# Gate rows, key roots and the gate bias of an attention layer: moved from the tail and from in front of attention into its first iteration, on one Trainium2 core

## The reference

```python
for i in range(DEPTH):
    mod = silu(c) @ w_ada[i] + b_ada[i]
    sh1, sc1, g1, sh2, sc2, g2 = split(mod, 6)
    h = rmsnorm(x, norm_mix[i]) * (1 + sc1) + sh1
    m = mla_mixer(h, ...) if i % 2 == 0 else rglru_mixer(h, ...)
    x = x + g1 * m
    h = rmsnorm(x, norm_ffn[i]) * (1 + sc2) + sh2
    x = x + g2 * moe(h, *route(h, ...), w_gu[i], w_dn[i])
```

## Time and profile before

| what | us |
|---|---|
| median of 3 runs | 1702.48 |
| fastest, slowest | 1700.49, 1705.16 |
| profiled execution | 1700.49 |
| span in the profile | 1698.7 |
| PE busy | 1384.3 (81%) |
| DVE busy | 686.6 (40%) |
| ACT busy | 347.9 (20%) |
| POOL busy | 296.6 (17%) |

### The profile page before, as it was taken

How to read it: one execution, slowest core, us unless ns; L and a number is a source line. 1 busy time by engine, 2 the same in 40 slices (tenths; PEclk the granted TensorE clock), 3 DMA queues, 4 the chain that set the end, 5 groups by cost and what they waited for, 6 DMA issues and landing times.

```text
span 1698.7 us, 33153 instructions
## 1 busy us (share of the span) xinstructions
PE 1384.3 (81%) x14067; PEld 803.0 (47%) x14067; DVE 686.6 (40%) x1316; ACT 347.9 (20%) x708; POOL 296.6 (17%) x340
## 2 busy tenths in 40 slices
PE   3999999989876777897757999797887768699754
PEld 3644554445644344485424444343564435377432
DVE  5677777766211111122205288757321112122113
ACT  3346555121100000001002345423010001001000
POOL 1001211000222032222100122200131222122200
PEclk9999999989988788999978999897998879899887
DMA  9654232599999999999996121066899999999997
GB/s 366 251 203 168 85 108 75 190 350 419 366 398 398 414 383 408 394 395 401 428 395 240 57 81 62 0 251 244 324 400 397 402 407 383 403 389 402 423 424 299
DMA packets 66841, 517.29 MB, mean 305 GB/s; under 512 B 13277, under 2 KB 26102, under 8 KB 49034
## 3 DMA queue, kind: packets, MB, share of 16 engines
q1 hardware_dynamic: 51696, 493.77, 73.2%
q0 software_dynamic: 10848, 16.24, 2.9%
q10 hardware_dynamic: 4154, 5.18, 0.9%
HBM read 506.27 MB, written 22.04 MB: 311 GB/s over the span
## 4 chain that ended last, share of the span: by engine, by line
PE 52%; DMA 33%; DVE 7%; another core or an unknown queue 2%; issue 2%; ACT 2%; SPq 1%; PEldq 1%; DVEq 0%; ACTq 0%
DMA ring_gu<-in_moe_w_gu_dram 29%; PE ps L1192 16%; PE ps L1199 6%; PE ps L1082 6%; DMA ring_gu<-in_w_ada_dram 4%; PE ps L1117 3%; PE ps L999 3%; PE ps L1101 2%; PE ps L909 2%; PE ps L1141 2%; PE ps L1019 2%; PE ps L973 2%; PE ps L889 2%; PE ps L937 2%
## 5 line engine op out<-in xcount | busy, mean ns | idle before, releaser
L1192 PE MATMUL ps<-ring_gu,arena 128*32 128x256 f32 x5248 | 359.5, 426 | 147.9 <-DMA ring_gu<-in_moe_w_gu_dram 131.7
L1192 PEld LDWEIGHTS ps<-ring_gu,arena 128*32 128x32 f32 x5248 | 204.4, 122 | 281.1 <-issue 107.4
L2093 DVE TENSOR_TENSOR arena<-arena,ps 128x128 f32<-128x128 f32 x120 | 34.4, 287 | 649.6 <-ACT arena L1620 634.6
L720 POOL DMA_INDIRECT ys_dram<-arena,out_idx x116 | 114.7, 989 | 662.4 <-DVE arena L2087 630.1
L1620 ACT ACTIVATE arena<-ps 128x128 f32<-128x128 f32 x120 | 33.3, 278 | 878.7 <-PE ps L1192 714.2
L1192 PE MATMUL ps<-arena 128*32 128x256 f32 x2432 | 165.5, 418 | 53.6 <-DMA arena<-in_moe_w_gu_dram 44.2
L1199 PE MATMUL ps<-ring_dn,arena 128*32 128x256 f32 x2624 | 173.7, 380 | 13.6 <-issue 10.1
L1192 PEld LDWEIGHTS ps<-arena 128*32 128x32 f32 x2432 | 105.4, 120 | 103.7 <-DMA arena<-in_moe_w_gu_dram 42.3
L713 POOL DMA_INDIRECT arena<-xn_dram,tok_idx x104 | 95.8, 921 | 279.4 <-issue 153.5
L1199 PEld LDWEIGHTS ps<-ring_dn,arena 128*32 128x32 f32 x2624 | 100.9, 110 | 69.3 <-issue 23.2
L1082 PE MATMUL ps<-arena 128*128 128x512 f32 x256 | 110.6, 592 | 0.2 <-ACT arena L1329 0.2
(11 more groups left out here) (359 smaller groups left out, 1541.8 us busy)
## 6 DMA issues: line engine op xcount, KB each, us to landing
ring_gu<-in_moe_w_gu_dram SPq DMA_DIRECT2D x44, 4096.0 KB
ring_dn<-in_moe_w_dn_dram SPq DMA_DIRECT2D x43, 2048.0 KB
arena<-in_moe_w_gu_dram SPq DMA_DIRECT2D x18, 4096.0 KB
arena<-in_moe_w_dn_dram SPq DMA_DIRECT2D x20, 2048.0 KB
...
```

The source lines that it names most:

```text
L720: g.indirect_dma_start(ys_dram, bass.IndirectOffsetOnAxis(ap=out_idx[:, col:col + 1], axis=0), yo[:, n % 4, :], None, bounds_check=2 * TIL ...
L1192: last = mm(ps[s_ * ROWS:(s_ + 1) * ROWS, pb, 0:2 * QF].rearrange("p (a b) -> p a b", a=2), rows[:, k, :], pair[:, :, s_, :], start=(k == ...
```

## The change

Five things move. The columns of the key/value projection are taken in their order in memory, so that each of the four groups holds keys and values of four heads; roots and reciprocals of the keys come in four groups of four heads. Of these, group 0 stays ahead of attention, the sums of groups 2 and 3 go into steps 0 and 4 of iteration 0, and the roots and reciprocals of groups 1 to 3 behind its step 7. POOL waits for them before head 4 instead of head 8. The gate rows go into steps 4 to 7 of iteration 0, all four in bank 7, each with its `gate_out` in the same step of DVE. The gate bias is loaded earlier, into another place. SP's wait for `gate_biased` goes from in front of the first stage rows to in front of `w_o`, which also waits for all four key sums. DVE's three `ada_row` of iteration 0 go from behind step 7 into step 3.

```diff
--- before.py
+++ after.py
@@ -141,7 +141,7 @@
 for _i in range(1, TT):
     _stage(f"q{_i}", "AAA")
 _stage("kv", "A" * 16, [0, 1, 2, 3, 4, 5, 6, 7, 2, 3, 4, 5, 6, 7, 6, 7])
-_stage("gate0", "DDDD", [2, 3, 4, 5])
+_stage("gate0", "DDDD", [7, 7, 7, 7])
 _project_and_route(0)
 _stage("cond1", "AAA", [3, 4, 5])
 _stage("rank0", "DD", [6, 7])
@@ -204,7 +204,7 @@
         ident = sb("ident", [P, P])
         ones = sb("ones", [P, P])
         before = sb("before", [P, P])
-        gate_bias = ring_gu0[0:1, 3072:3072 + 2 * D]
+        gate_bias = ring_gu1[0:1, 6144:6144 + 2 * D]
         vrows = arena[0:NVROW, 0:P]
         vcols = sb("vcols", [P, NVROW])
         brows = arena[0:48, P:2 * P]
@@ -284,7 +284,7 @@
         kT = view(ring_dn0, 1792, 2, SEQ)
         rope_tmp = view(ring_gu1, 0, 4, TT * H * RH)
         sq_tmp = view(ring_dn0, 0, 2, H * QK)
-        sq_kv = view(ring_gu1, 4096, 2, 2 * H * NOPE)
+        sq_kv = view(ring_gu1, 4096, 2, H * NOPE)
         lat_sq_tmp = view(arena, 16896, QL)
         mla_small = sb("mla_small", [P, 576])
         trig = arena[:, 17408:17408 + 5 * TT * RH].rearrange("p (n i j) -> p n i j", n=5, i=TT)
@@ -534,10 +534,9 @@
                 if l == 0:
                     sp.wait_ge(S["ada_used"], 12)
                     for r in range(2 * KT):
-                        if r == 0:
+                        if r == 1:
+                            sp.wait_ge(S["sq_used"], 2 * TT)
                             sp.wait_ge(S["gate_biased"], 1)
-                        if r == 1:
-                            sp.wait_ge(S["sq_used"], TT + 2)
                             sp.dma_start(w_o, mla_w_o[0].rearrange("(k p) n -> p k n", p=P)).then_inc(S["w_o_in"], 16)
                         for j in range(3):
                             if r:
@@ -676,10 +675,10 @@
                                 ALU.mult).then_inc(S["qkn_ready"], 1)
 
             head_inputs(0)
-            with pool.Fori(1, 8) as h:
+            with pool.Fori(1, 4) as h:
                 head_inputs(h)
-            pool.wait_ge(S["rope_done"], 3)
-            with pool.Fori(8, H) as h:
+            pool.wait_ge(S["rope_done"], TT + 1)
+            with pool.Fori(4, H) as h:
                 head_inputs(h)
 
             g.memset(acc1_next, 0.0).then_inc(S["acc1_zero"], 1)
@@ -933,16 +932,13 @@
                 g = STAGES["kv"] + 4 * n + i
                 pe.wait_ge(*emptied(before_in_bank(g)))
                 for k in range(2):
-                    heads = w_kvb[:, k, :].rearrange("p (h d) -> p h d", h=H)[:, n % 2 * H // 2:(n % 2 + 1) * H // 2, :]
-                    last = mm(bank(g), latT[:, 3 + k, i * P:(i + 1) * P],
-                              heads[:, :, 0:NOPE] if n < 2 else heads[:, :, NOPE:NOPE + VH],
+                    last = mm(bank(g), latT[:, 3 + k, i * P:(i + 1) * P], w_kvb[:, k, n * HALF:(n + 1) * HALF],
                               start=(k == 0), stop=(k == 1))
                 last.then_inc(S["unit"], 1)
 
             def gate_row(n):
                 g = STAGES["gate0"] + n
                 pe.wait_ge(*emptied(before_in_bank(g)))
-                pe.wait_ge(S["p_ready"], NSTEP - TT + n + 1)
                 pe.wait_ge(S["gate_biased"], 1)
                 mm(bank(g), ones[:, :], gate_bc[:, n // 2, n % 2 * HALF:(n % 2 + 1) * HALF],
                    start=True, stop=True).then_inc(S["unit"], 1)
@@ -1025,10 +1021,13 @@
                 if p < TT:
                     kv_unit(3, p)
                     pe.wait_ge(*emptied(STAGES["kv"] + 4 * 2 + p))
+                else:
+                    gate_row(p - TT)
                 if p == 3:
                     pe.wait_ge(*emptied(STAGES["kv"] + 4 * 3 + 2))
                 head_step(0, p)
             pe.wait_ge(*emptied(STAGES["kv"] + 15))
+            pe.wait_ge(*emptied(STAGES["gate0"] + 3))
             for it in range(1, H // 2 - 1):
                 for p in range(8):
                     head_step(it, p)
@@ -1036,9 +1035,6 @@
                 head_step(H // 2 - 1, p, last_pair=True)
             for p in range(4):
                 head_step(H // 2, p, tail=True)
-                if p < TT - 1:
-                    gate_row(p)
-            gate_row(TT - 1)
 
             pe.wait_ge(S["o_done"], H // 2)
             pe.wait_ge(S["w_o_in"], 16)
@@ -1377,43 +1373,36 @@
                     act.wait_ge(S["lam_abs"], 1)
                     A(lam_t[:, 1, :], lam_t[:, 0, :], ACT.Exp, scale=-1.0).then_inc(S["lam_exp"], 1)
             q_tile_out(0)
+            act.wait_ge(S["ada_used"], 8)
+            act.dma_start(gate_bias.rearrange("o (s n) -> o s n", n=D), b_ada[0:1, :].rearrange("o (s n) -> o s n", n=D)[:, 2:6:3, :]
+                          ).then_inc(S["brow_in"], 16)
             latT_out(TT - 1)
             for i in range(1, TT):
                 q_tile_out(i)
 
             def rk_std(n):
                 act.wait_ge(S["qk_var"], n + 2)
-                A(rk[:, :, 8 * n:8 * n + 8], rk[:, :, 8 * n:8 * n + 8], ACT.Sqrt, bias=eps[:, :], scale=1.0 / QK
+                A(rk[:, :, 4 * n:4 * n + 4], rk[:, :, 4 * n:4 * n + 4], ACT.Sqrt, bias=eps[:, :], scale=1.0 / QK
                   ).then_inc(S["qk_std"], 1)
 
             def kv_out(n, i):
                 g = STAGES["kv"] + 4 * n + i
                 act.wait_ge(S["unit"], g + 1)
-                heads = kv_tok[:, :, n % 2 * H // 2:(n % 2 + 1) * H // 2, :]
-                part = heads[:, i, :, 0:NOPE] if n < 2 else heads[:, i, :, NOPE:NOPE + VH]
-                A(part, bank(g).rearrange("p (h d) -> p h d", h=H // 2), ACT.Copy,
+                A(kv_tok[:, i, 4 * n:4 * n + 4, :].rearrange("p h d -> p (h d)"), bank(g), ACT.Copy,
                   scale=lat_r[:, 1, i:i + 1]).then_inc(S["a_free"], 1)
-                if n < 2 and i == TT - 1:
+                if i == TT - 1:
                     act.wait_ge(S["a_free"], evacuated(g)[1])
-                    for half in range(2):
-                        hs = slice(4 * half, 4 * half + 4)
-                        sq = sq_kv[:, n, :].rearrange("p (i h d) -> p i h d", i=TT, h=H // 2)
-                        last = A(sq[:, :, hs, :], heads[:, :, hs, 0:NOPE], ACT.Square)
-                    last.then_inc(S["sq_ready"], 1)
+                    head_squares(TT + n, sq_kv[:, n % 2, :].rearrange("p (i h d) -> p i h d", i=TT, h=4),
+                                 kv_tok[:, :, 4 * n:4 * n + 4, 0:NOPE])
 
             for n in range(3):
                 for i in range(TT):
                     kv_out(n, i)
                 if n == 0:
-                    act.wait_ge(S["ada_used"], 12)
-                    act.dma_start(gate_bias.rearrange("o (s n) -> o s n", n=D), b_ada[0:1, :].rearrange("o (s n) -> o s n", n=D)[:, 2:6:3, :]
-                                  ).then_inc(S["brow_in"], 16)
                     act.wait_ge(S["qk_var"], 1)
                     A(rq, rq, ACT.Sqrt, bias=eps[:, :], scale=1.0 / QK).then_inc(S["qk_std"], 1)
                 if n == 1:
                     rk_std(0)
-                if n == 2:
-                    rk_std(1)
 
             def q_out(h, hb):
                 act.wait_ge(S["qkT_made"], h + 1)
@@ -1451,6 +1440,8 @@
                 if p < TT:
                     kv_out(3, p)
                 head_step(0, p)
+            for n in range(1, 4):
+                rk_std(n)
             with act.Fori(1, H // 2 - 1) as it:
                 for p in range(8):
                     head_step(it, p)
@@ -1812,16 +1803,16 @@
             dve.wait_ge(S["qk_std"], 1)
             v.reciprocal(rq, rq).then_inc(S["rope_done"], 1)
             def rk_sums(n):
-                group = rk[:, :, 8 * n:8 * n + 8]
+                group = rk[:, :, 4 * n:4 * n + 4]
                 dve.wait_ge(S["sq_ready"], TT + n + 1)
-                v.tensor_reduce(group, sq_kv[:, n, :].rearrange("p (i h d) -> p i h d", i=TT, h=H // 2),
+                v.tensor_reduce(group, sq_kv[:, n % 2, :].rearrange("p (i h d) -> p i h d", i=TT, h=4),
                                 AX.X, ALU.add).then_inc(S["sq_used"], 1)
                 dve.wait_ge(S["sq_used"], TT + n + 1)
-                v.tensor_tensor(group, group, pe_ss.rearrange("p (i o) -> p i o", o=1).to_broadcast([P, TT, 8]),
+                v.tensor_tensor(group, group, pe_ss.rearrange("p (i o) -> p i o", o=1).to_broadcast([P, TT, 4]),
                                 ALU.add).then_inc(S["qk_var"], 1)
 
             def rk_inverse(n):
-                group = rk[:, :, 8 * n:8 * n + 8]
+                group = rk[:, :, 4 * n:4 * n + 4]
                 dve.wait_ge(S["qk_std"], n + 2)
                 v.reciprocal(group, group).then_inc(S["rope_done"], 1)
 
@@ -1858,7 +1849,7 @@
                 v.scalar_tensor_tensor(out=acc1[ch], in0=stage[:, j, :], scalar=c_act[:, at(k)], in1=acc1[ch],
                                        op0=ALU.mult, op1=ALU.add).then_inc(S["stage_used"], 1)
 
-            def head_step(it, p, last_pair=False, tail=False, rows_late=False):
```

(22 more changed lines are left out.)

## The result

| | before | after |
|---|---|---|
| median of 4 runs, us | 1703.78 | 1720.63 |
| lowest, highest | 1700.49, 1705.16 | 1718.47, 1721.32 |
| span in the profile | 1698.7 | 1714.3 |
| PE busy | 1384.3 | 1363.5 |

The ratio is 1.0092, with a 95% interval from 1.0073 to 1.0111: about 15.7 us slower (12.4 to 18.9; the two medians of four runs differ by 16.9). The direction was forecast; the time lies 3.6 us above the top of the range, and the growth is over twice the 7.1 us of the sum.

What follows compares the result with a forecast made beforehand. It took engines waiting for each other as the bound before 300 us, largely bytes after 320. +0.1 + 9.9 + 0.1 - 2.95 = +7.1 on 1700.5 gave 1707.6, as median 1709.6, written 1710; range 1704 to 1717.

Steps and rivals of the forecast that it cites:

- the sum: Whole kernel: opening +0.1, iteration 0 +9.9, table load back to Exp +0.1, tail -2.95, together +7.1 us; chance 0.47.
- rival 1: Iteration 0: PE's clock falls to half while it waits, +3 to +6 us, time 1713.6; chance 0.23.
- PE's gate rows go: about 0: Tail of attention: removing PE's gate rows changes about 0, since they lay in holes between transposes.
- Tail, -2.95: Behind attention: without gate copies DVE comes 2.95 us earlier, and this reaches the end; bounds -0.3 and -6.
- the forecast's lower bound: Tail: gain of only -0.3 us if expert 0's load, hanging on PE's last unit, sets the stream.
- Iteration 0, +9.9: Steps 3 to 7: closed PE-DVE hand-overs, then table load and roots, delay iteration 1's first maximum by 9.9 us; bounds +4, +14.
- expected spacing of the gate products: Iteration 0: gate products at 3.3, 5.5 and 3.5 us spacing, PE waiting for DVE's gate copy.
- Rival 2: Turn to the experts: the clock stays up since the gap before 365.55 closes, time 1706.5; chance 0.16.
- Rival 3: Stage rows land late, or each loop turn gets a table load: +2 to +4 us, time 1712.5; chance 0.05.
- Rival 4: ACT's table switches hold it longer than the load, 1.28 us each for two: +2.6, time 1712.2; chance 0.03.
- Rival 5: Gates fill an existing PE hole in iteration 0, costing 0.5 us; kernel faster, 1697 to 1700; chance 0.06.
- Layout, bias, `w_o`: Opening and loads: layout +0.1 us, gate bias 0, `w_o` issued at about 163.0 with r=1 rows in time, 0.

Runs made afterwards that it cites:

- gates moved alone: Kernel before with only the gate rows moved, into steps 4 to 7 of iteration 0, bank 7, each copied out by DVE in that step; ratio 1.0054.
- the second profile: The changed kernel, unaltered, run and profiled once more beside the follow-up kernels; ratio to the kernel before 1.0089.
- gates back: The changed kernel with its gate rows returned to the tail, banks 2 to 5, copied out behind it; ratio to the kernel before 1.0037.
- roots alone: Kernel before with the change's key/value layout, key roots, early gate bias and SP order; gate rows in the tail, `ada_row` behind step 7; ratio 1.0045.
- rows spread: Kernel before with iteration 0's three `ada_row` placed one behind each of steps 0, 1 and 2; ratio 0.9982.
- PE filled: The changed kernel plus unread PE products behind steps 4, 5 and 6 of iteration 0 and each tail step; ratio to the kernel before 1.0044.
- copied first: Kernel before with only the gate rows moved into iteration 0, DVE copying each gate ahead of the step's row maximum; ratio 1.0023.
- rows late: The changed kernel with iteration 0's three `ada_row` back behind step 7, after the reciprocals; ratio to the kernel before 1.0091.
- The two kernels with ACT's copies: Kernel before with tail gate copies by ACT instead of DVE, ratio 0.9987; the same plus iteration 0's `ada_row` in steps 0 to 2, ratio 0.9981.

## Why the prediction missed, point by point

**The step that failed: rival 1 taken for a rival, at 0.23, when it is the likeliest course.** The forecast wrote that a gap of 3.21 us was followed by half clock and one of 2.88 us was not the earlier trace rows, computed 3.8 us for the new gap, and concluded that "the rows decide neither way". By the length of the gap they leaned: 3.8 lies beyond both, on the side of the one that fell. But two rows were thin ground, and the length alone doesn't decide: with the gates moved alone the clock fell behind gaps of at most 2.19 us. The fall came in both profiles of the change (gap 3.63 us) and in all six kernels that lengthened iteration 0 with PE unfilled. Its price, +3 to +6 with 4.0 taken (1713.6 less 1709.6), measured 3.4 (13.63 less 10.19) and, in the second profile, 4.3. Even with it the forecast was 7 us short of the median, and 4.6 short of the growth (11.1 against 15.7).

The Trainium skill (TensorE: Matmul & The Clock Gate, "HAM oscillation") warns of idle gaps of TensorE between bursts, and the trace agrees (3.63 us, then 0.50), though a gap that long was not needed for a fall (2.19 us, above). It also has "A second HAM failure mode", in which many short idles between groups of products do the same, there in a kernel that goes through its PSUM banks in turn; that fits the tail, where no gap was over 0.87 us.

**"PE's gate rows go: about 0" was wrong: +1.7 to +3.0.** They cost nothing in the tail's holes, true, but they kept the clock up for the products behind them. Each kernel without them, and without fill, took 7.4 to 9.0 us for the stretch; all with gate rows or fill there 6.01. Nothing in the forecast asked what the clock would do where work of PE is removed.

**Tail, -2.95: the mechanism came, the size stays open.** DVE came earlier by as much as forecast, the gap before the tile logits closed to 1.87 us and expert 1's load came 3.5 us earlier. Against the profile of before, 1.3 to 1.5 us were left at the first expert product, and from the projection's start to the end the change takes 1.5 us less in one profile and 0.4 more in the other. That looks like the forecast's lower bound, -0.3 "if the load of expert 0, which hangs on PE's last unit, sets the stream", and the load of expert 0 indeed stands 59.7 us behind the projection's start in 12 of the 13 profiles. But the one profile of before is early here too. Where DVE still copies the gates behind the tail (before, gates back, roots alone, rows spread), the projection's start to the end takes 1396.0, 1396.6, 1399.6 and 1398.8 us; in the six profiles where it doesn't (both of the change, gates moved, PE filled, copied first, rows late) 1393.8 to 1396.4. The means differ by 2.9 us, those of the first expert product by 3.3. The two kernels with ACT's copies (1396.5 and 1404.2) speak against it. The scatter is as large as the term, so neither -2.95 nor -0.3 is shown; that PE filled came out at +7.5 against the sum of +7.1 favours the first.

**Iteration 0, +9.9, and the table loads: right.** +10.19 at full clock against 10.1. The expected spacing of the gate products (3.3, 5.5, 3.5) can be read only where the clock stayed: 3.37 us and 5.5 in gates moved alone (164.09 less 160.72, 169.58 less 164.09). The third can't be seen: behind step 7's gate row no other follows.

**Rival 2** (the clock stays up in the turn) came in part: 4.04 us for the conditioning products instead of 4.48, clock 0.92 from 384 to 388. Whether it gave time at the end can't be told from these runs. **Rival 3** had a true mechanism and no price: each turn of the loop now holds a table load. It stands behind ACT's wait for the first maximum (0.68 us, before 0.70), so it delays the first Exp; ACT makes that up from its waits in the next three steps, and the turn stays at 18.08 us; the rows of r=1 were used at 188.33 without a wait. **Rival 4** fell: the Exp at 184.39 follows its load by 0.02 us, and so does the first Sqrt at 181.17 by 0.01; so the drain that the Trainium skill adds (ScalarE: Activation LUTs, "What ACT_TABLE_LOAD costs") shows in neither. **Rival 5** fell too: iteration 0 grew, and the tail gave nothing to set against it.

**Layout, bias, `w_o`: as forecast.** The bias had no wait, `w_o` went at 164.95 (forecast 163.0, plus the 1.8 us by which this profile runs later).

The new sum: hand-overs +10.2, clock in iteration 0 +3.4 to +4.3, clock in the tail +1.7 to +3.0, behind it -1.5 to +0.4: +13.8 to +17.9, against 15.7 measured. With the forecast's -2.95 as the last term it is +12.4 to +14.6, at the lower end of the measured interval (12.4 to 18.9). What isn't resolved is that last term, which is as large as the spread between profiles; the two terms of the clock are what the forecast lacked.
